# Column-wise roots and reciprocals in the norms of a two-block transformer forward pass on one core

## The reference, cut to what matters

```python
def rms_norm(t, gain):
    y = tf * lax.rsqrt(jnp.mean(tf * tf, axis=-1, keepdims=True) + NORM_EPS)
    return y * gain
def layer_norm(x, g, b):
    mu = jnp.mean(xf, axis=-1, keepdims=True)
    var = jnp.mean(jnp.square(xf - mu), axis=-1, keepdims=True)
    return (xf - mu) * lax.rsqrt(var + LN_EPS) * g + b
...
h = rms_norm(x, attn_norm[i]) * (1.0 + sc_a) + sh_a
o = rms_norm(o, out_norm) * (1.0 - lam_init)
h = layer_norm(alpha * h + g1 * y, ln_g[l, 0], ln_b[l, 0])
```

## Time and profile before

| what | us |
|---|---|
| median of three executions | 2285.18 |
| lowest and highest | 2284.11, 2288.91 |
| the profiled execution | 2283.09 |
| its span, first to last instruction | 2281.2 |
| PE busy | 2208.6 (97% of the span) |
| DVE busy | 1860.9 (82%) |
| ACT busy | 1343.0 (59%) |
| mean granted clock of PE, share of full speed | 0.993 |

### The profile page before, as it was taken

How to read it: one execution, slowest core, us unless ns; L and a number is a source line. 1 busy time by engine, 2 the same in 40 slices (tenths; PEclk the granted TensorE clock), 3 DMA queues, 4 the chain that set the end, 5 groups by cost and what they waited for, 6 DMA issues and landing times.

```text
span 2281.2 us, 31881 instructions
## 1 busy us (share of the span) xinstructions
PE 2208.6 (97%) x13055; PEld 1926.5 (84%) x13055; DVE 1860.9 (82%) x2353; ACT 1343.0 (59%) x1513; POOL 69.2 (3%) x103
## 2 busy tenths in 40 slices
PE   4999999999999999999999999999999999999997
PEld 3888999888999868999697888888888888888885
DVE  7966888875998667888765888888898888888897
ACT  3564433574443766433631777777777777776774
POOL 0000111000000000010000000000000000000000
PEclk9999999999999999999999999999999999999999
DMA  9745888625787616885543699999999999999991
GB/s 376 278 185 194 330 313 298 221 75 195 278 304 276 217 38 222 323 319 208 212 157 139 223 363 360 350 360 360 347 365 346 362 350 365 346 368 350 359 364 53
DMA packets 259039, 635.78 MB, mean 279 GB/s; under 512 B 9191, under 2 KB 21384, under 8 KB 258184
## 3 DMA queue, kind: packets, MB, share of 16 engines
q1 hardware_dynamic: 234376, 539.30, 64.8%
q0 software_dynamic: 24512, 94.38, 10.9%
HBM read 632.60 MB, written 1.05 MB: 278 GB/s over the span
## 4 chain that ended last, share of the span: by engine, by line
PE 83%; DVE 9%; DMA 2%; ACT 2%; issue 1%; POOL 0%; ACTq 0%; DVEq 0%
PE ps L1172 81%; DVE wring_rounded L2824 3%; DVE aring L2851 2%; DMA aring<-in_ada_rows 2%; PE ps L2122 1%; PE ps L1336 1%; DVE work L2824 1%; DVE OT L2848 1%; DVE X L2831 1%; ACT scr_rounded L2180 0%; PE ps L1311 0%; DVE H L2824 0%; DVE work_rounded L2824 0%; DVE X L2824 0%; DVE rstd L2914 0%
## 5 line engine op out<-in xcount | busy, mean ns | idle before, releaser
L2824 DVE TENSOR_TENSOR wring_rounded<-wring,scr_rounded 128x2048 fp32r<-128x2048 f32 (+1 forms) x314 | 568.5, 1838 | 79.2 <-ACT scr_rounded L2180 79.1
L2180 ACT ACTIVATE scr_rounded<-wring 128x2048 fp32r<-128x2048 f32 (+1 forms) x314 | 480.0, 1553 | 196.8 <-PE ps L1172 131.2
L1172 PE MATMUL ps<-wring_rounded,OT_rounded 128*128 128x512 f32 (+1 forms) x1184 | 316.4, 392 | 5.0 <-ACT OT_rounded L2187 2.4
L1172 PEld LDWEIGHTS ps<-wring_rounded,OT_rounded 128*128 128x128 f32 x1184 | 221.1, 189 | 51.0 <-ACT wring_rounded L2180 5.3
L2824 DVE TENSOR_TENSOR wring_rounded<-wring,H_rounded 128x2048 fp32r<-128x2048 f32 (+1 forms) x85 | 193.2, 2273 | 26.6 <-ACT H_rounded L2180 26.5
L2851 DVE CUSTOM_DVE_ANT_0 aring<-aring,F,vec 128x1024 f32<-128x1024 f32 x152 | 187.7, 1280 | 32.4 <-DMA aring<-in_ada_rows 31.7
L2824 DVE TENSOR_TENSOR wring_rounded<-wring,aring_rounded 128x2048 fp32r<-128x2048 f32 x84 | 192.2, 2289 | 16.2 <-ACT aring_rounded L2180 16.2
L2180 ACT ACTIVATE H_rounded<-wring 128x2048 fp32r<-128x2048 f32 (+1 forms) x85 | 162.4, 1910 | 61.3 <-issue 39.8
L2180 ACT ACTIVATE aring_rounded<-wring 128x2048 fp32r<-128x2048 f32 x84 | 161.2, 1919 | 57.8 <-PE ps L1172 57.8
L1172 PE MATMUL ps<-V_rounded,wring_rounded 128*128 128x256 f32 x1184 | 179.1, 286 | 4.4 <-DVE wring_rounded L2824 4.3
L1172 PE MATMUL ps<-work_rounded,F_rounded 128*128 128x256 f32 x1056 | 169.8, 283 | 0.0
(11 more groups left out here) (342 smaller groups left out, 3745.2 us busy)
## 6 DMA issues: line engine op xcount, KB each, us to landing
wring<-in_moe_gate SPq DMA_DIRECT2D x56, 2048.0 KB, 7.9
wring<-in_moe_up SPq DMA_DIRECT2D x56, 2048.0 KB, 8.6
wring<-in_moe_down SPq DMA_DIRECT2D x56, 2048.0 KB, 8.0
aring<-in_ada_rows POOLq DMA_DIRECT2D x88, 1024.0 KB, 7.6
wring<-in_ffn_w_gate SPq DMA_DIRECT2D x10, 2048.0 KB, 9.5
wring<-in_ffn_w_up SPq DMA_DIRECT2D x10, 2048.0 KB, 14.1
wring<-in_ffn_w_down SPq DMA_DIRECT2D x10, 2048.0 KB, 10.2
wring<-in_diff_w_in SPq DMA_DIRECT2D x6, 2048.0 KB, 14.3
```

Source lines behind the costliest of these rows:

```text
L1172: return pe.matmul(dst, lhsT, rhs, start=start, stop=stop, **kw)
L2180: return act.activation(dst, src, ACT.Copy, **kw)
L2824: return ve.tensor_tensor(dst, x, y, op)
```

## The change

Every root and reciprocal of the numbered norms and of the heads is taken of one column per 128 tokens (`ncol`, 128x2; `hcol`, 128x16 for eight heads). The squares become the stationary operand of two products per tile, whose moving operand is one column of ones (`by_token_sum`); the bank is cleared first by a zero product (`clear`). After the reciprocal two products of the column's broadcast and the identity write the factors as 128x256 rows to a bank of PSUM of their own (`spread_inverse`, banks by `plan_norm(..., spread=)`), and the scalings read them there. That spread stands at a fixed place in PE's order: after the clearing products of a feed-forward and ahead of five idle products (nine before), in norm 2 after three and ahead of five idle products (eight before), in norm 6 after six and ahead of four (18 before), in norm 5 directly after the sums and ahead of the taps products, in norms 0 and 7 directly after the sums. In norms 4, 6 and 7 the mean of the remainder is summed a second time, by columns, and three small DVE operations take its square off. For the heads, ACT takes the root of heads 0 to 6 in the middle of the last attention units, and PE spreads the first two heads ahead of the last head's sum; the seven idle products there go.

The diff, cut (the same edit of the scalings in norms 0 and 5, the other `plan_norm` calls, semaphores and a table of counts are left out):

```diff
@@ -356,7 +356,7 @@
-        rheads = rstd[0:32, :]
+        ncol, hcol = sb("ncol", [P, 4]), sb("hcol", [P, 2 * KT])
...
@@ -463,10 +463,11 @@
-        norm_job = []
-        def plan_norm(*banks):
+        norm_job, norm_spread = [], []
+        def plan_norm(*banks, spread):
...
+            norm_spread.append(J(spread))
         def plan_units(groups):
...
@@ -508,7 +509,7 @@
-        plan_norm(6)
+        plan_norm(6, spread=7)
...
@@ -1186,50 +1188,73 @@
+            def clear(job):
+                job.open(pe)
+                mm(PS[job.b][:, :], zero[:], con[:, 0:2 * P].bitcast(BF16), True, False)
+            def by_token_sum(job, x, at, stop=False):
+                for qt in range(2):
+                    last = mm(PS[job.b][:, at + qt:at + qt + 1], x[:, qt * P:(qt + 1) * P], C("ones")[:, 0:1],
+                              False, stop and qt == 1)
+                return last
             def sum_squares(n):
...
+                clear(job)
+                if n in (0, 5):
+                    tiles = range(KT)
+                else:
+                    pe.wait_ge(norm_sums, summed(n))
+                    by_token_sum(job, H[:, 0, :], 0)
+                    tiles = range(4 if n == 2 else SOLO + 1, KT)
+                for k in tiles:
+                    pe.wait_ge(sq_tile, KT * n + k + 1)
+                    last = by_token_sum(job, H[:, k, :], 0, k == KT - 1)
+                fill(job, last)
+            def spread_inverse(n):
+                job = norm_spread[n]
...
-                if n in (0, 5):
-                    for k in range(KT):
-                        pe.wait_ge(sq_tile, KT * n + k + 1)
-                        last = mm(PS[job.b][:, 0:T], C("ones"), H[:, k, :], k == 0, k == KT - 1)
-                    fill(job, last)
-                    return
-                pe.wait_ge(norm_sums, summed(n))
-                mm(PS[job.b][:, 0:T], C("ones"), H[:, 0, :], True, False)
-                for k in range(4 if n == 2 else SOLO + 1, KT):
-                    pe.wait_ge(sq_tile, KT * n + k + 1)
-                    last = mm(PS[job.b][:, 0:T], C("ones"), H[:, k, :], False, k == KT - 1)
+                pe.wait_ge(norm_inverse, n + 1)
+                for qt in range(2):
+                    last = mm(PS[job.b][:, qt * P:(qt + 1) * P], ncol[:, qt:qt + 1].to_broadcast([P, P]), C("ident"))
...
             def sum_late(n):
...
-                sq.open(pe)
+                clear(sq)
...
+                by_token_sum(sq, rstd[:], 2)
...
-                mm(PS[sq.b][:, 0:T], C("ones"), H[:, 0, :], True, False)
+                by_token_sum(sq, H[:, 0, :], 0)
...
+                by_token_sum(sq, X[:, KT - 1, :], 2)
...
-                fill(sq, mm(PS[sq.b][:, 0:T], C("ones"), H[:, KT - 1, :], False, True))
+                fill(sq, by_token_sum(sq, H[:, KT - 1, :], 0, True))
             def sum_last():
...
-                sq.open(pe)
+                clear(sq)
...
+                        by_token_sum(sq, rstd[:], 2)
...
+                        by_token_sum(sq, X[:, k, :], 2)
...
-                    last = mm(PS[sq.b][:, 0:T], C("ones"), H[:, k, :], k == 0, k == KT - 1)
+                    last = by_token_sum(sq, H[:, k, :], 0, k == KT - 1)
...
             def sum_tiles(n, jobs):
...
@@ -1454,11 +1479,11 @@
             def feed_forward(f, L, after={}):
-                L["y"][0].open(pe)
-                idle_products(4, 9)
...
-                    job.open(pe)
-                    mm(PS[job.b][:, :], zero[:], con[:, 0:2 * P].bitcast(BF16), True, False)
+                    clear(job)
+                spread_inverse(FFN_NORM[f])
+                L["gj"][0].open(pe)
+                idle_products(0, 5)
...
@@ -1559,7 +1585,9 @@
-            idle_products(1, 8)
+            idle_products(1, 3)
+            spread_inverse(2)
+            idle_products(1, 5)
...
@@ -1573,25 +1601,31 @@
             def head_sum(t):
...
-                    on_stat.open(pe)
+                    clear(on_stat)
...
-                last = mm(PS[on_stat.b][:, 0:T], C("whole")[:, 32 - t:32 - t + P], H[:, t, :], t == 0, t == KT - 2)
+                last = by_token_sum(on_stat, H[:, t, :], 2 * t, t == KT - 2)
...
-            on_last.open(pe)
+            clear(on_last)
+            def spread_heads(j):
+                on_bc[j].open(pe)
+                for t in (2 * j, 2 * j + 1):
+                    pe.wait_ge(rh_ready, 2 if t == KT - 1 else 1)
+                    for qt in range(2):
+                        o = t % 2 * T + qt * P
+                        last = mm(PS[on_bc[j].b][:, o:o + P], hcol[:, 2 * t + qt:2 * t + qt + 1].to_broadcast([P, P]), C("ident"))
+                fill(on_bc[j], last)
+            spread_heads(0)
...
-            fill(on_last, mm(PS[on_last.b][:, 0:T], C("ones"), H[:, KT - 1, :]))
-            idle_products(1, 7)
-            pe.wait_ge(rh_ready, 1)
-            for j in range(4):
-                on_bc[j].open(pe)
-                for t in range(2 * j, min(2 * j + 2, KT - 1)):
-                    last = mm(PS[on_bc[j].b][:, t % 2 * T:(t % 2 + 1) * T],
-                              C("ident")[0:32, t:t + 1].to_broadcast([32, P]), rheads)
-                fill(on_bc[j], last)
+            fill(on_last, by_token_sum(on_last, H[:, KT - 1, :], 0, True))
+            for j in range(1, 4):
+                spread_heads(j)
             def difference_weights(c):
...
@@ -1803,6 +1837,7 @@
+            spread_inverse(5)
...
@@ -1940,7 +1975,9 @@
-            idle_products(6, 18)
+            idle_products(6, 6)
+            spread_inverse(6)
+            idle_products(6, 4)
...
@@ -2172,6 +2209,7 @@
+            spread_inverse(7)
...
@@ -2198,16 +2236,13 @@
             def deviation(n):
+                job = norm_job[n][-1]
...
-                    _, dev, sq = norm_job[n]
-                    sq.filled(act)
-                    act.activation(H[:, 1, :], PS[dev.b][:, 0:T], ACT.Square, scale=1.0 / 32).then_inc(norm_roots, 1)
-                    sq.emptied(act)
-                    root(rstd[:], rstd[:], D, C("ln_eps")).then_inc(norm_roots, 1)
+                    job.emptied(act)
+                    root(ncol[:, 0:2], ncol[:, 0:2], D, C("ln_eps")).then_inc(norm_roots, 1)
...
-                job = norm_job[n][-1]
...
-                root(rstd[:], PS[job.b][:, 0:T], D, C("ln_eps" if n >= 4 else "rms_eps")).then_inc(job.bank.free, 1)
+                root(ncol[:, 0:2], PS[job.b][:, 0:2], D, C("ln_eps" if n >= 4 else "rms_eps")).then_inc(job.bank.free, 1)
             def shifted(n, shift, upper=None):
...
@@ -2262,9 +2297,15 @@
-            def head_root(job, n, rows=32):
+            def head_root(job, lo, hi):
...
-                root(rheads[0:rows, :], PS[job.b][0:rows, 0:T], n, C("rms_eps", rows)).then_inc(job.bank.free, 1)
+                root(hcol[:, lo:hi], PS[job.b][:, 0:hi - lo], P, C("rms_eps")).then_inc(job.bank.free, 1)
+            def early_roots():
+                act.activation(warm[:], C("ones")[:, 0:1], ACT.Sqrt)
+                head_root(on_stat, 0, 2 * KT - 2)
             def units(plan, specs, base, place, pv_base, between={}, squared=False, part=False):
...
@@ -2476,10 +2517,8 @@
-                  {18: lambda: act.activation(warm[:], C("ones")[:, 0:1], ACT.Sqrt)}, True)
-            head_root(on_stat, P)
-            on_last.filled(act)
-            root(H[:, 0, :], PS[on_last.b][:, 0:T], P, C("rms_eps")).then_inc(on_last.bank.free, 1)
+                  {18: early_roots}, True)
+            head_root(on_last, 2 * KT - 2, 2 * KT)
...
@@ -2911,7 +2950,17 @@
             def inverse(n):
...
-                step(ve.reciprocal(rstd[:], rstd[:]))
+                ve.reciprocal(ncol[:, 0:2], ncol[:, 0:2]).then_inc(norm_inverse, 1)
+            def inverse_rows(n):
+                norm_spread[n].filled(ve)
+                return PS[norm_spread[n].b][:, 0:T]
+            def rows_read(n):
+                ve.wait_ge(scaled, KT * n + KT)
+                ve.sem_inc(norm_spread[n].bank.free, 1)
             def centre(n, k):
...
@@ -2970,8 +3019,10 @@
             def rms(n, sh=None, upper=None):
...
+                root = inverse_rows(n)
...
-                    stt(H[:, k, :], X[:, k, :], gsc[:, k:k + 1], rstd[:], ALU.mult, ALU.mult).then_inc(scaled, 1)
+                    stt(H[:, k, :], X[:, k, :], gsc[:, k:k + 1], root, ALU.mult, ALU.mult).then_inc(scaled, 1)
+                rows_read(n)
...
@@ -3003,29 +3054,27 @@
-                ve.wait_ge(norm_roots, ROOTS[n] + 1)
-                tt(rstd[:], PS[sq.b][:, 0:T], H[:, 1, :], ALU.subtract).then_inc(sq.bank.free, 1)
+                step(ts(ncol[:, 2:4], PS[sq.b][:, 2:4], 1.0 / 32, ALU.mult))
+                step(tt(ncol[:, 2:4], ncol[:, 2:4], ncol[:, 2:4], ALU.mult))
+                tt(ncol[:, 0:2], PS[sq.b][:, 0:2], ncol[:, 2:4], ALU.subtract).then_inc(sq.bank.free, 1)
...
+                ve.wait_ge(norm_roots, ROOTS[n])
+                ve.reciprocal(ncol[:, 0:2], ncol[:, 0:2]).then_inc(norm_inverse, 1)
...
```

(42 more changed lines are left out.)

6 lines of the change are left out of this document (4 added, 2 removed).

## The result

The changed kernel takes 2287.28 us (median of 20 runs, 2284.61 to 2292.16), the kernel before 2283.94 us beside it (20 runs): a ratio of 1.0016, 95% interval 1.0009 to 1.0022, so about 3.7 us **slower**. Forecast were 2282.9 us, a little faster (2.3 us under the 2285.18 of three runs; the median of 20 is 1.2 us lower). The profiled execution took 2288.3 us, its span 2286.5.

A forecast was written before the change was run, and what follows sets the result against it. The prediction took the chain of waits, 83% TensorE, as the bound. Path terms of -4.2 us and a clock term of +1.95 gave -2.25 on the profiled execution, 2282.9 us against the median of 2285.18; range 2276 to 2289.

The forecast's parts named there:

- the clock term: Norms 1, 2, 4, 5 and heads: low clock behind thin products beside gaps, less what is given back, +1.95 us together.
- -0.75 + 1.2: Norm 1: shorter path from root to first product, -0.75 us; low clock slowing products before the feed-forward, +1.2.
- -0.7 + 0.75 - 1.2: Norm 2: scaling earlier by 0.7 us, low clock costing 0.75, and 1.2 given back as its PE gap closes.
- 1.25 + 1.3 - 0.5: Heads' norm: spread ends 1.25 us earlier, the 64 products behind gain 1.3, low clock on full-row spreading costs 0.5.
- half of the taps' 3.7 us, 1.8: Norm 5: a low clock behind one-column sums and the new wait costs 1.8 us on the filter taps.
- 1.45: Norm 5: the spread ahead of the filter taps waits for the reciprocal and delays them, +1.45 us, 1.2 to 1.75.
- one-column products won't take longer there: Norm 7: at the low clock only the spread takes longer, by 0.4 us; the norm gains 0.5.
- the router's thin products bring the clock down: Behind norm 6, at 1258 to 1259 us: low clock after the router's eight-column products, without a gap; no size given.
- A: Whole kernel: only gaps lower the clock, thin sums keep it; -6.7 us, 2278.5 us, chance 0.25.
- C: Feed-forward starts: low clock at spreads of norms 1, 3 and 4, more at 2, 5 and heads; +6.2, 2291.4 us, chance 0.10.
- D: Scalings in eight norms: reading the factor from PSUM costs 0.065 us more each; 2287.0 us, chance 0.03.
- E: Before 400 us: shifts meet a nearly full DMA queue and waits elsewhere replace them; -0.5, 2284.7 us, chance 0.12.

The follow-up runs named there:

- experiment 12: The kernel before with the heads' norm alone in its new form: 2280.41 us, ratio 0.9986 to the kernel before.
- experiment 4: The changed kernel with all by-token sums 128 columns wide (the heads' 32), one column read: 2277.44 us, ratio 0.9965 to the kernel before.
- experiments 8: The changed kernel with eight never-executed zero products in the untaken branch ahead of norm 7: 2284.20 us, ratio 0.9999 to the kernel before.
- experiment 9: The kernel before with 121 never-executed zero products in the untaken branch ahead of norm 7: 2288.06 us, ratio 1.0019 to the kernel before.
- experiment 3: The changed kernel with norm 5's spread moved between the two filter taps: 2287.41 us, ratio 1.0011 to the kernel before.
- experiments 5: The changed kernel with norm 5's sums alone 128 columns wide: 2282.16 us, ratio 0.9985 to the kernel before.
- 6: The changed kernel with a 128x512 zero product behind each of the first seven one-column pairs of norm 5's sums: 2283.49 us, ratio 0.9995 to the kernel before.
- 11: The changed kernel with all sums wide and eight never-executed zero products in the untaken branch: 2273.65 us, ratio 0.9953 to the kernel before.

## Why the prediction was wrong

Most path terms were right; the clock term, norm 7 and what was left out had the wrong size, and with them the sign of the whole. Leads are taken between traces, from the first product ahead of a norm to the first behind it.

- **Norms 1 to 4 and the heads: right, the heads too small.** Norm 1 gained 0.9 us without a low clock (-0.75 + 1.2 forecast), norm 3 about 0.9 (0.75). Norm 2 gained 1.2, from a lead of 4.3 to 5.4, with the low clock that was forecast for it: -0.7 + 0.75 - 1.2 = -1.15. The heads gained 2.8 us here (3.2 by the ratio of experiment 12) for the forecast's 1.25 + 1.3 - 0.5: the product at 517.14 ahead of them is at 511.72, a lead of 5.4, and the 64 products start 527.45 - 520.55 = 6.9 us earlier, so the start moved by 1.5 for 1.25; they went from 9.33 to 8.02 us as foreseen, and the 0.5 for slower spreading was not needed. Norm 4 gained about 0.7 for 0.8. The clock terms of norms 1 and 4 (1.2, 0.2) were not needed: of the seven traces with one-column products there, the clock was low at norm 1 in one and at norm 4 in none. At norm 2 it was low in three of the seven, the changed kernel's own among them.
- **Norm 5, the step that failed: "half of the taps' 3.7 us, 1.8".** The direction was right, loss by the spread ahead of the taps and a low clock; the size was 8.0 us for 1.45 + 1.8 = 3.25. The clock fell within the sums (2.06 us more for them), and the taps lost not half but all, 7.19 - 3.70 = 3.5 us, and the 64 products behind them 1.5 more. The 1.45 of the order came to 0.9 in experiment 4. The forecast had given the reason itself, thin products beside a gap, and then priced it as if the low clock ended with them.
- **Norm 7, the second failed step: "one-column products won't take longer there".** They do: 28 records take 5.97 us for 4.87, and the clock stays low to the end where it rose before, so that the sums of the last tile and the spread behind them run at half speed. Minus 0.5 was forecast, plus 3.6 measured, 3.3 of which go with wide sums (experiment 4). That the clock rose within the old sums (14 records in 4.87) was to be read in the earlier trace rows and was taken as fixed.
- **What no term held: the branch.** 4.3 us of standstill more: 3.3 of them are the second wait for instructions, by where the code lies, as experiments 8 and 9 show in both kernels; the other 1.0 lies within what the first standstill varies by between kernels without a second (2.6 to 4.3). Nothing in the trace of before showed that its 2.98 us were the good case.
- **Norm 6: right.** Its first router product starts 0.9 us earlier, as forecast, and the lead grows by 2.5 in all. The rest is the low stretch at 1257 to 1261 that isn't there after. By this, the reading of the earlier trace rows that the router's thin products bring the clock down was at best half of it: with the same products the clock stayed full. It was low there in all three traces with norm 6 in its old form and in three of the eleven with the new one. The reading that the heads' 32-row spreads bring it down fits better: it was low behind them in both traces that have them, and there in none of the twelve others.
- **The rivals.** A (only gaps count) falls: experiment 4 has the changed kernel's waits ahead of its sums and a full clock in them, and experiment 3 has no gap behind its sums and a low one. C put the low clock at the feed-forwards' starts, where it wasn't in the changed kernel's trace; its time, 2291.4, was too high, but its kind, a low clock beyond the thin products, is what happened, at norms 5 and 7. D (PSUM readings) falls with 0.476 for 0.479; that its 2287.0 is nearly the measured time is chance. E (the gain is absorbed) falls too: the early lead lasted to norm 5 and was lost there by a slower clock. The range, 2276 to 2289, held the result, and "the same", within 0.2%, was the likeliest case and came true with 1.0016; both owe something to luck, since the sum had the wrong sign and losses of 15.9 us stood against gains of 10.5.

In sum, in the profiled executions: a lead of 8.0 us up to norm 5, 8.0 lost in norm 5, 2.5 won in norm 6, 3.6 lost to the clock and 4.3 to the branch in norm 7; 8.0 - 8.0 + 2.5 - 3.6 - 4.3 = -5.4, and the spans differ by 5.3. Between the profiled executions the distance is larger than by the ratio, 3.7 us.

That the Trainium skill ("TensorE: Matmul & The Clock Gate", section on HAM oscillation) ties the fall of the clock to gaps between bursts agrees in kind with experiments 5, 6 and 11, where it fell at or behind a wait, though the waits here, 0.65 to 1.24 us, are shorter than those of the section's example. It doesn't cover the changed kernel and experiment 3, where it fell inside the sums with TensorE busy since their start, and where the same wait of 0.96 us ahead of 128-column sums left it full.

**What stays open.** The lead ahead of norm 2 varies between executions of the same instructions there: in experiment 12's trace, which has the old code up to the heads, TensorE is there up to 3.4 us behind the kernel before, and in experiment 9's, which executes the same instructions up to norm 7, it is 2.5 us ahead from norm 2 to norm 6. So a part of the early lead of 5 us may be chance; the gains of the single norms are firmer. Why a given gap triggers the clock in some executions and not in others wasn't tried, nor whether the wait in norm 5 would do it without taps of 64 rows behind it. Nor was the pitch of the bad code placements: seen are six kernels at the changed kernel's position with a second standstill, one 4 instructions ahead of it with a shorter one, and kernels 14 and 16 behind and 42, 188 and 246 ahead without.

## What to carry to other kernels

A sum by products of one column takes about as long as one of 128 columns here (16 records of one column 1.84 us, 32 of 128 columns 3.84, 0.12 each), but behind a wait of about 1 us it brought the clock down where 128 columns did not: keep the columns and read one. Where a serial step is shortened, look at what TensorE does meanwhile, since with a wait of 0.65 to 1.24 us behind sums that ran at full clock, norm 5 cost 4.0 to 7.4 us in three of four profiles and 0.9 in the fourth. And before a result of some tenths of a per cent is put down to an edit, compare the standstills behind branches and the instruction transfers in them: padding that is never executed moved this kernel by 0.2%.

## What the runs showed of the hardware

- Thin products and the clock: 32 one-column records behind a gap of about 1 us brought the granted clock to 0.50 within 2 us of their start in every kernel that had them in norm 5 without filling (four profiles); the same sums at 128 columns never did (four profiles).
- Behind a branch, TensorE stands still for 2.6 to 4.3 us at good places of the code, and for 5.5 to 7.3 us at others, in two parts of which the second is 2.7 to 3.3 us, with a weight load or a product between them; in experiment 9 the second is 1.7. The profile puts both down to "issue", and each ends 1.3 to 2.0 us after a 16 KB transfer of queue q8, kind "instruction", has ended.
- Once low in norm 5, the clock stayed so for 17 us, through taps that use 64 rows with TensorE busy all the time (1.00 busy, 0.50 granted from 1086 to 1094), and came back 3 to 4 us after products of full 128 rows had begun at 1093.9. In norm 7 it did not come back in 11 us of products, nearly all of one column, at full busy time; with 128 columns (experiment 4) it came back within the sums, at 2263.2.
